# An even layer's recurrence that hands a state from chunk to chunk instead of scoring every pair of chunks

## What is computed

```python
A = einsum('bhtd,bhsd,bhtsd->bhts', qb, kb, decay)       # inside a chunk
o = einsum('bhts,bhsv->bhtv', A, vb)
o = o + einsum('bhtd,bhdv->bhtv', qb * exp(Gb), state)   # from earlier chunks
k_dec = kb * exp(g_last[:, :, None, :] - Gb)
state = exp(g_last)[..., None] * state + einsum('bhsd,bhsv->bhdv', k_dec, vb)
```

## Time and profile before

| | |
|---|---|
| median of 3 runs | 1134.72 us (1133.17 to 1135.48) |
| the profiled execution | 1133.06 us, its span 1131.2 us |
| busy, of the span | PE 98%, PEld 80%, DVE 85%, ACT 61% |
| projections (L74 to L76, `bank_proj`) on PE | 856 passes each line, 340.4 + 334.2 + 334.4 us |
| 128x512 fp32 products with the values (L500) on PE | 128 passes |
| granted TensorE clock | 0.998 of full speed over the span |

### The profile page before, as it was taken

One profiled execution on the slowest core, in us unless ns is written; L12 is line 12 of the kernel. 1 busy time (PEld: TensorE's weight loads), 2 busy tenths in 40 slices (PEclk: granted clock), 3 DMA queues, 4 the chain that ended last, 5 costly groups with the idle time before them and its releaser, 6 DMA issues. The chain is left out here.

```text
span 1131.2 us, 18238 instructions
## 1 busy us (share of the span) xinstructions
PE 1103.6 (98%) x5560; PEld 905.7 (80%) x5560; DVE 965.2 (85%) x1971; ACT 684.5 (61%) x1326; POOL 0.2 (0%) x4
## 2 busy tenths in 40 slices
PE   7999999999999999999999999999999999999996
PEld 6778778778778778778778777787888888888875
DVE  6889889889889889889889799789888888888886
ACT  6475565565565565565565584276667766667764
POOL 0000000000000000000000000000000000000000
PEclk9999999999999999999999999999999999999999
DMA  7614423323323323323323320453432324333111
GB/s 228 168 37 115 128 75 83 104 74 84 102 74 86 99 74 90 96 74 91 94 74 91 95 75 19 120 150 76 130 93 56 93 56 112 92 95 93 56 39 75
DMA packets 131531, 103.67 MB, mean 92 GB/s; under 512 B 5409, under 2 KB 116385, under 8 KB 131489
## 3 DMA queue, kind: packets, MB, share of 16 engines
q1 hardware_dynamic: 131344, 102.87, 33.2%
q10 hardware_dynamic: 144, 0.26, 0.1%
HBM read 77.95 MB, written 2.10 MB: 71 GB/s over the span
## 5 line engine op out<-in xcount | busy, mean ns | idle before, releaser
L74 PE MATMUL bank_proj<-hH,w_hi 128*128 128x512 f32 x856 | 340.4, 398 | 1.1 <-issue 0.6
L76 PE MATMUL bank_proj<-hH,w_lo 128*128 128x512 f32 x856 | 334.4, 391 | 0.0
L75 PE MATMUL bank_proj<-hL,w_hi 128*128 128x512 f32 x856 | 334.2, 390 | 0.0
L76 PEld LDWEIGHTS bank_proj<-hH,w_lo 128*128 128x128 f32 x856 | 160.7, 188 | 34.7
L74 PEld LDWEIGHTS bank_proj<-hH,w_hi 128*128 128x128 f32 x856 | 161.0, 188 | 32.7 <-issue 1.1
L75 PEld LDWEIGHTS bank_proj<-hL,w_hi 128*128 128x128 f32 x856 | 161.1, 188 | 30.6 <-issue 0.2
L2012 ACT ACTIVATE probs<-probs,small 128x256 f32<-128x256 f32 (+1 forms) x128 | 70.9, 556 | 51.6 <-DVE small L2271 51.4
L1258 DVE TENSOR_TENSOR w_lo<-w_raw,w_hi 128x1024 fp32r<-128x1024 f32 x74 | 89.6, 1219 | 0.8 <-ACT w_hi L741 0.7
L2019 ACT ACTIVATE probsT<-bank_odd_turn 128x256 fp32r<-128x256 f32 (+1 forms) x128 | 48.8, 434 | 65.0 <-PE bank_odd_turn L1735 64.4
L741 ACT ACTIVATE w_hi<-w_raw 128x1024 fp32r<-128x1024 f32 x74 | 77.9, 1053 | 0.2
L868 ACT ACTIVATE scaled<-decay 128x1024 f32<-128x1024 f32 x32 | 33.9, 1059 | 70.5 <-PE bank_score L584 68.5
(11 more groups left out here) (448 smaller groups left out, 2148.7 us busy)
## 6 DMA issues: line engine op xcount, KB each, us to landing
w_raw<-in_w_in_even SPq DMA_DIRECT2D x72, 512.0 KB, 4.9
w_raw<-in_w_in_odd SPq DMA_DIRECT2D x36, 512.0 KB, 4.9
qs<-parts SPq DMA_DIRECT2D x96, 128.0 KB, 2.3
ks<-parts SPq DMA_DIRECT2D x40, 256.0 KB, 4.3
o_raw<-in_w_out_even SPq DMA_DIRECT2D x15, 512.0 KB, 6.3
o_raw<-in_w_out_odd SPq DMA_DIRECT2D x14, 512.0 KB, 6.7
mixT<-in_x SPq DMA_DIRECT2D x2, 512.0 KB, 5.9
attT<-in_x SPq DMA_DIRECT2D x2, 512.0 KB, 6.7
```

The source lines that it names most:

```text
L74: pe.matmul(out, hi, moving_hi, start=start, stop=False)
L75: pe.matmul(out, hi, moving_lo, start=False, stop=False)
L76: return pe.matmul(out, lo, moving_hi, start=False, stop=stop)
```

## The change

The score matrix of different chunks is gone. In its place, for each direction, the decayed keys of three chunks are transposed (`turn_keys`), copied back by ScalarE (`keep_turned`), multiplied by the values into one 128x128 state contribution for each chunk (`states`), and added up with their decays (`keep_state` copies the first, `step_states` makes the second and third on VectorE). `far_scale` is two products of 384 columns into `query_in`. `recurrence_values` is ten products of 128 columns: values by the diagonal scores for each chunk, and state by decayed query for three chunks in each direction, accumulated in bank `O`. `attT` is divided anew (diagonal scores 512 columns, states 768, queries 768). Every transpose and state uses the score banks, `S[1]` for three uses in a row. The order of several steps moves on all three engines.

```diff
@@ TensorE
-            def far(h, x):
...
-                for col, key, qry in products:
-                    mm = pe.matmul(bank[:, col * P:col * P + qry.shape[1]], key, qry, start=True, stop=True)
+            def turn_keys(h, d):
+
+                pe.wait_ge(far_exp.sem, far_exp.at(h, 6))
+                pe.wait_ge(S[1].free.sem, S[1].free.at(h, 4 + d))
+                for c in range(3):
+                    mm = pe.transpose(S[1][:, c * P:(c + 1) * P], scaled[:, d, 1, c * P:(c + 1) * P], eye[:])
+                mm.then_inc(S[1].full.sem, 1)
+
+            def states(h, d):
+
+                pe.wait_ge(S[1].free.sem, S[1].free.at(h, 5 + d))
+                if d == 0:
+                    pe.wait_ge(S[1].free.sem, S[1].free.at(h, 6))
+                else:
+                    pe.wait_ge(S[0].free.sem, S[0].free.at(h, 5))
+                bank = S[1 - d]
+                for c in range(3):
+                    mm = pe.matmul(bank[:, c * P:(c + 1) * P], scaled[:, d, 0, c * P:(c + 1) * P], vh[:, c + d, :],
+                                   start=True, stop=True)
                 mm.then_inc(bank.full.sem, 1)
...
-                values(h, 1, vh, att)
+                for c in range(NC):
+                    cols = O[:, c * P:(c + 1) * P]
+                    mm = pe.matmul(cols, vh[:, c, :], att_diag[:, c], start=True, stop=False)
+                    if c > 0:
+                        mm = pe.matmul(cols, state[:, 0, c - 1], query_in[:, 0, (c - 1) * P:c * P], start=False,
+                                       stop=c == NC - 1)
+                    if c < NC - 1:
+                        mm = pe.matmul(cols, state[:, 1, c], query_in[:, 1, c * P:(c + 1) * P], start=False, stop=True)
...
+                turn_keys(h, 0)
+                diagonal(h)
+                turn_keys(h, 1)
+                if first:
+                    pe.wait_ge(T.free.sem, T.free.at(h, 6))
+                    values(h, 6, v, mixT)
+                else:
+                    out_tiles(h, range(4, 6))
+                states(h, 0)
+                states(h, 1)
                 if not first:
-                    out_tiles(h, range(4, 8))
-
-                diagonal(h)
-                pe.wait_ge(T.free.sem, T.free.at(h, 6))
-                values(h, 6, v, mixT)
-                far(h, 1)
-                far(h, 2)
-                far(h, 3)
+                    out_tiles(h, range(6, 8))
+                    pe.wait_ge(T.free.sem, T.free.at(h, 6))
+                    values(h, 6, v, mixT)
+                proj(h, 7, 2 if first else 0, 4)
                 sum_squares(h, 7, 2)
-                proj(h, 7, 2 if first else 0)
-                near_level(h, 0)
+                if not first:
+                    near_level(h, 0)
+                proj(h, 7, 4)
+                if first:
+                    near_level(h, 0)
                 near_level(h, 1)
@@ ScalarE
                 if first:
                     keep_mix(h, 3)
+                    keep_turned(h, 0)
                 else:
                     keep_mix(h, 2)
                 if last:
                     keep_mix(h, 3)
+                    keep_turned(h, 0)
+                    keep_turned(h, 1)
                 silu(h, 6, gate_a)
                 act.preload_act_table_set(EXP_LOG)
                 if not first and not last:
                     keep_mix(h, 3)
-                if not first:
-                    high_out(h, 0)
+                    keep_turned(h, 0)
...
+                keep_turned(h, 1)
+                if first:
+                    square(h, 6, 2)
+                keep_state(h, 0)
+                near_decays(h, 0)
+                keep_state(h, 1)
+                near_decays(h, 1)
                 if not first:
+                    high_out(h, 0)
                     high(h, 9)
-                square(h, 6, 2)
-                keep_far(h, 1)
-                near_decays(h, 0)
-                keep_far(h, 2)
-                near_decays(h, 1)
-                keep_far(h, 3)
+                    square(h, 6, 2)
@@ VectorE
+            def step_states(h, d):
...
+                dve.wait_ge(bank.full.sem, bank.full.at(h, use))
+                dve.wait_ge(state_kept.sem, state_kept.at(h, d + 1))
+                dve.scalar_tensor_tensor(out=state[:, d, two], in0=state[:, d, one], scalar=by(1 + d), in1=fresh(two),
+                                         op0=ALU.mult, op1=ALU.add).then_inc(state_stepped.sem, 1)
...
-                if not first:
-                    add_out(h, range(4, 8))
                 place_diagonal(h)
                 near_differences(h, 0)
+                if not first:
+                    add_out(h, range(4, 6))
+                    step_states(h, 0)
+                    step_states(h, 1)
                 near_differences(h, 1)
                 if not first:
+                    add_out(h, range(6, 8))
+                    near_scale(h, 0)
                     low_out(h, 0)
```

More of the change, by code:

```diff
@@ L670, in end_of_last @@
             def end_of_last(h):
+                turn_keys(h, 0)
                 diagonal(h)
-                far(h, 1)
-                far(h, 2)
+                turn_keys(h, 1)
                 pe.wait_ge(T.free.sem, T.free.at(h, 6))
-                values(h, 6, v, mixT, 0, 1)
-                far(h, 3)
+                values(h, 6, v, mixT, 0, 2)
+                states(h, 0)
+                states(h, 1)
                 out_tiles(h, [4])
                 near_level(h, 0)
-                values(h, 6, v, mixT, 1, 2)
                 near_level(h, 1)
@@ L847, in far_decays, with keep_turned, keep_state @@
                 act.activation(scaled[:, 1, 1, 0:3 * P], keys[:, 1, P:4 * P], ACT.Exp).then_inc(far_exp.sem, 1)
[L849 to L853, removed]
-                        2: (S[0], 6, (1, 2, 4, 0), (2, 0, 2, 2)),
-                        3: (S[1], 6, (3, 0, 3, 0), (1, 0, 1, 3))}
-                bank, use, one, two = jobs[x]
+            def keep_turned(h, d):
+                act.wait_ge(S[1].full.sem, S[1].full.at(h, 5 + d))
+                act.activation(scaled[:, d, 0, 0:3 * P], S[1][:, 0:3 * P], ACT.Copy).then_inc(S[1].free.sem, 1)
+            def keep_state(h, d):
+                bank, use = (S[1], 7) if d == 0 else (S[0], 6)
+                if O.full.due(h, 1):
+                    act.wait_ge(O.full.sem, O.full.at(h, 1))
                 act.wait_ge(bank.full.sem, bank.full.at(h, use))
-                for (s, t0, t1, col), count in ((one, far_kept), (two, bank.free)):
-                    act.activation(att[:, s, t0 * P:t1 * P], bank[:, col * P:(col + t1 - t0) * P],
-                                   ACT.Copy).then_inc(count.sem, 1)
+                act.activation(state[:, d, 2 * d], bank[:, 2 * d * P:(2 * d + 1) * P],
+                               ACT.Copy).then_inc(state_kept.sem, 1)
             def near_decays(h, i):
@@ L872, in place_blocks @@
                 b, bank = 1 << ORDER[i], S[i % 2]
-                act.wait_ge(bank.full.sem, bank.full.at(h, 7))
+                act.wait_ge(bank.full.sem, bank.full.at(h, near_use(i)))
                 if i == 0:
@@ new lines, in step_states @@
+            def step_states(h, d):
+                bank, use = (S[1], 7) if d == 0 else (S[0], 6)
+                one, two, three = (0, 1, 2) if d == 0 else (2, 1, 0)
+                fresh = lambda c: bank[:, c * P:(c + 1) * P]
+                by = lambda c: total[:, d, c:c + 1]
+                dve.wait_ge(bank.full.sem, bank.full.at(h, use))
+                dve.wait_ge(state_kept.sem, state_kept.at(h, d + 1))
+                dve.scalar_tensor_tensor(out=state[:, d, two], in0=state[:, d, one], scalar=by(1 + d), in1=fresh(two),
+                                         op0=ALU.mult, op1=ALU.add).then_inc(state_stepped.sem, 1)
+                dve.wait_ge(state_stepped.sem, state_stepped.at(h, d + 1))
+                dve.scalar_tensor_tensor(out=state[:, d, three], in0=state[:, d, two], scalar=by(2 - d),
+                                         in1=fresh(three), op0=ALU.mult, op1=ALU.add).then_inc(bank.free.sem, 1)
```

78 lines of the change are left out of this document (37 added, 41 removed).

## The result

The changed kernel takes **1151.29 us**, the median of 4 executions from 1147.15 to 1152.74, against 1135.10 us for the kernel before on the same chip: 1.0138 times as long, 95% interval 1.0108 to 1.0168. The forecast was 1144.5 us, slower, with 1137.5 to 1151 as its range; the direction holds, and the median lies 0.3 us above the range's end (the kernel before was 0.4 us slower here, too, than the 1134.72 that the forecast started from).

A forecast was written before the change was run, and what follows sets the result against it. TensorE was taken to bound heads 0 to 6, VectorE's chain of levels head 7. Savings and new waits summed to +9.9 us on the profiled 1133.06, 1143.0; with the median 1.7 above, 1144.5 us, range 1137.5 to 1151.

The forecast's parts named there:

- TensorE's own work: TensorE's removed and added instructions per head: 0.91 us less in mid-head, 1.20 us less at the next head's start.
- The dearer transposes: New transposes read `scaled` instead of `mix`; at a product's price they cost 0.67 us more per head.
- First wait: Heads 1 to 6: the second `turn_keys` waits for ScalarE's `keep_turned(h, 0)`; TensorE pauses 2.3 us, until 155.38.
- Second wait: Heads 1 to 6: the attention's values wait for VectorE's addition of output tile 7; pause 1.55 us, start 164.04.
- Behind these: After both pauses: projection 8 at 175.2 instead of 172.45, VectorE 0.1 us behind it, later levels not worse served.
- rival 3: VectorE becomes the bound in the levels; 1.8 us behind projection 8's start would give 1150.5 us; chance 10%.
- Steady head: Distance from one head's diagonal to the next: 86.4 us forecast, 84.6 us before.
- Head 0: Saves 0.91 us, pauses 0.35 at the second `turn_keys`, and late weights hold projection 8 by 0.85: +0.3 us.
- Head 7: Bound by VectorE's chain of levels, which begins about 1.1 us later; TensorE's saving goes into waits: +0.3 us.
- The sum: +17.7 us mid-head in heads 1 to 6, -8.4 recurrence's values, +0.3 and +0.3 in the outer heads: +9.9 us.
- Rival 4, the clock: TensorE's clock falls in the pauses: 12 pauses, each followed by 2.7 us at half speed, +32 us, 1177; chance 3%.
- my signs of being wrong: A steady head under 84.6 us, a gap at a level's products, or a clock under 1.0 in a steady head.

The follow-up runs named there:

- the other two edits: Projection 7's passes ahead of the attention's values, and level 2's Exp and scaling ahead of the norm, added to ScalarE's early copy in the changed kernel: 1123.28 us.

## Why the prediction was right, and where it fell short

- **TensorE's own work**: held. The ten products with the values take 2.23 us by starts (202.20 to 204.35, and 0.08 in the next row), six states 1.25 to the next row's start (1.34 predicted), three key transposes 0.33. The dearer transposes kept for the range did not come.
- **First wait**: predicted until 155.38, measured 155.22, and 2.25 us long for 2.3. It came from reading ScalarE's queue behind projection 6. The table load is again 1.28 us with the next copy 0.01 us behind it.
- **Second wait**: predicted 164.04 and 1.55 us, measured 164.11 and 1.6. The step of 128 columns was 0.35 us instead of 0.30.
- **Behind these**: projection 8 predicted at 175.2, measured 175.31, VectorE's scaling of level 2 at 175.44 for 175.3, no level of heads 1 to 6 served late; rival 3 did not come in the changed kernel. It came in the experiments, where the pauses that hid it were gone.
- **Steady head**: predicted 86.4 us, measured 86.3. Head 0: pauses of 0.30 and 0.77 for 0.35 and 0.85. Head 7: levels wait 2.2 us in all instead of 0.5, and what lies outside the seven diagonal distances is 0.7 us longer for 0.3.
- **The sum**: +9.9 us for the profiled execution; measured +14.1, of which 3.2 are its two falls of the clock. Without them 1144.0 for 1143.0.
- **Rival 4, the clock**: this is the step that fell short. I held it to be one case with 3%, all pauses or none, at 2.7 us each: 32 us. The runs show it in part: in the profile the clock falls behind two first pauses and no second one; by the mean clocks an execution has two to about six falls, 1.6 us each. That is about the difference between 1144.5 and the median of 1151.3. A clock under full in a steady head was also one of my signs of being wrong, and heads 3 and 5 showed it. I had taken the trace's word that waits of up to 1.5 us leave the clock full and had then let it stand for a new wait of 2.3, longer than any of its kind in mid-span. The Trainium skill, page "TensorE: Matmul & The Clock Gate", section "HAM oscillation — how this bites in real kernels", says that repeated idle gaps of TensorE make the clock drop and that each drop is paid for in slow work behind the gap; the run with waits of 3.0 us agrees in every head, the changed kernel in some, the run with the projection ahead in none. The gaps of that section's own example are longer than either pause here, so the section by itself didn't put a price on them, as the prediction's "by that rule" has it. The term ought to have been 6 pauses by a chance by about 1.6 us, 0 to 10 us, added to the range's upper end.

## What to carry to other kernels

Before an instruction of the bounding engine is put behind one of another engine, read that engine's queue up to it, table loads included: two lines moved on ScalarE turned 1.4% slower into no change, and the other two edits made it 1% faster. Count a saving on the bound engine only with the second engine's slack beside it: here VectorE, 85% busy, took 0.7 of 2.25 us per head back until its own order was changed. And give a recurring wait of TensorE of 2 us or more a range above its own length, for slow passes behind it that may or may not come: waits of 2.1 us cost some 7 us more than their length in one order of the steps and nothing in another.

## What the runs showed of the hardware

- TensorE's clock fell to half behind waits of 2.1 us in some heads and not in others of the same execution, with the same work on either side, behind waits of 3.0 us in all six, behind none of six waits of 2.1 us with the second pause away, and now and then behind 1.5 or 1.6 or two of 0.9 and 0.8 close together; each fall in a steady head was over after some nine passes of 512 columns and cost 1.6 us. What decides it below 3.0 us stays open.
- Work that nobody needs, put in such a wait, kept the clock full: with nine idle passes in each first pause the mean clocks were 0.997 and 0.998 for 0.990 to 0.995, and the median 5.5 us lower.
- At the program's start TensorE's passes of 512 columns were 0.42 us apart until about 16 us in two of the traced executions and 0.23 from 12 us on in the others, for 2.0 and 2.5 us of the whole time.
- A VectorE step of 128 columns with two tensors and a column, one of them in PSUM, takes 0.35 us, against 0.28 for 128 columns by a column.
